# A two-block fp32 kernel: a transfer order, three instruction orders and four DRAM sums are moved

## The chip, the cores and the metric

The kernel runs on one core of one Trainium2 chip. The metric is the device time of one execution in microseconds, here the median of three runs.

## The reference

Two transformer-like blocks work on 256 tokens of width 2048, in fp32. Cut to its products:

```python
# block 1
proj = rmsnorm(x) @ w_in                  # 2048 x 8200
y = concat(mlstm(proj[...]), hgrn2(proj[...]))
h = x + y @ w_out
h = h + sigmoid(rmsnorm(h) @ w_pg) * (p @ w_pe)
x = rmsnorm(h)
# block 2
proj = rmsnorm(x) @ w_in_2                # 2048 x 9216: u, v, q, k, v_att, g_a, g_b
y_a, y_b = spatial_gating(u, v), stick_breaking_attention(q, k, v_att)
merged = sigmoid(g_a) * (y_a @ w_up_a) + sigmoid(g_b) * (y_b @ w_up_b)
x = x + merged @ w_o
hid = rmsnorm(x) @ w_ffn_in               # 2048 x 11264, then silu(gate) * up
x = x + (silu(gate) * up) @ w_ffn_out
x = x + sigmoid(rmsnorm(x) @ w_ple_gate) * (p_2 @ w_ple)
```

## The kernel before, in words

**Pieces.** All weights stream once through the core, in 848 numbered pieces. A piece is 256 rows by 512 columns of a weight (512 KB). Each piece passes three engines: ScalarE rounds it into `whi` (`split_hi`, L928, or `s_hi`, L1177), VectorE makes the rest `wlo = piece - whi` (L1876, or `s_lo`, L2556), and TensorE multiplies with high and low parts of the activations. A standard piece (`piece`, L1359 and L1364) is 8 matmuls on `whi` and 4 on `wlo`, for all 256 tokens. `whi` and `wlo` are rings of four pieces, `raw` is a ring of eight: ScalarE can be at most four pieces ahead of TensorE, and a load can start when the VectorE step that last read its place is done (`lo_ready`).

**Groups.** Most of the gates of block 2 and of the FFN input (12 groups: 0 to 2 in the merge, 3 to 11 in the FFN) are multiplied in a Strassen-like form of seven products of half size, M1 to M7, of four pieces each. The order is M1, M2, M7, M5, then M6 and M3 mixed, then M4. A piece of these has 4 matmuls on `whi` (L1724) and 2 on `wlo` (L1728). Standard pieces are mixed in.

**Where their weights come from.** M1's four pieces come into `r1` in two loads of 1 MB (L774). M5's come into the same `r1`, over M1's, in two loads of 1 MB (`fifth`, L780), from sums that lie in DRAM. M2, M7 and M3 take single 512 KB loads into four half-slots (L788): `b21`, `seventh` (sums from DRAM) and `b22`. M6's piece is `r1` plus `b22`, added on VectorE two pieces ahead (`s_sum`, L2551). M4's piece is `r1` plus `b21`: GpSimd issues an accumulating DMA into `r1` for it (L898) once M6's low part of that quarter is made.

**The order of the loads.** SyncE issues all loads in one order. For the second half it is the list `PLAN.loads`, sorted by (`free`, `need`): the piece whose `wlo` must be made first, and the piece that needs it. SyncE waits for each `free` in turn. `plan_s_loads` (L259 to L271) writes the entries of the groups.

**DRAM sums.** 48 sums of two weight tiles (1 MB each), four per group, are made in DRAM. SyncE issues a copy of the first term (L671, in `copies_for_sums`, ahead of the first load whose `need` reaches the entry of `SUM_AT`), GpSimd an accumulating DMA of the second (L882, in `add_in_dram`, once TensorE has used as many pieces as the entry says). Sums 0 to 39 are spread over pieces 24 to 269. Sums 40 to 43 stand at `g_plan + 1 + 4 * i` (pieces 277, 281, 285, 289) and 44 to 47 at `g_out + 11 + 6 * i` (419, 425, 431, 437). `g_plan` is 276, `g_out` 408, `g_ffn` 440. Group 3 starts at piece 458. Sums 40 to 47 belong to groups 10 and 11.

**The other places.** `ml_cols` on TensorE (L1484 to L1498) makes four small transposes and then spreads four rows over 128 partitions, two matmuls for each of two PSUM banks, with an operand of four partitions (L1497); VectorE reads both banks in `ml_weights`. On VectorE, the step at weight piece `L0 + 30` multiplies one half of the HGRN2 output by its norm (L2251, in front of the HGRN2 steps of the other half), and `u_product` (L2592, L2595) multiplies an up-projection with its gate, three pieces after the last piece of the slab.

Of the kernel before, what the change touches and what calls it, by code (L numbers as in the profile page):

```python
# [39 lines left out]
S = 256  # L40
# [82 lines left out]
class Plan:  # L123
# [129 lines left out]
    def plan_s_loads(self, groups):  # L253

        n = self.halves
        for c in groups:
            at = lambda i: self.s_at[(c, *S_ORDER[i])]
            for h in range(2):
                free = {0: self.g_plan + 9, M_GROUPS: self.g_block}.get(c)  # L259
                free = self.s_at[c - 1, "M4", 2 * h + 1] if free is None else free  # L260
                self.loads.append((free, self.s_at[c, "M1", 2 * h], "r1", h, c))
                self.loads.append((self.s_at[c, "M1", 2 * h + 1], self.s_at[c, "M5", 2 * h], "fifth", h, c))
            for i, (m, q) in enumerate(S_ORDER):
                for what, first, last in (("b21", "M2", "M2"), ("b22", "M6", "M3"), ("seventh", "M7", "M7")):
                    if m == first:
                        slot = RAW // 2 + n % 4
                        need = at(i - S_LEAD if m == "M6" else i)
                        self.loads.append((self.last_use[slot], need, "half", slot, (c, what, q)))
                        self.half[c, what, q] = (slot, 16 * (n // 4 + 1))
                        self.last_use[slot] = self.s_at[c, last, q]  # L270
                        n += 1  # L271
        self.halves = n
# [42 lines left out]
def two_blocks_kernel(nc, A, out):  # L315
    PLAN = Plan()
    SLABS, FIRST, S_AT = PLAN.slabs, PLAN.first, PLAN.s_at
    AUX = plan_aux()
    ctx = ExitStack()
    with ctx:  # L320
# [143 lines left out]
        summed = nc.dram_tensor("summed", (4 * S_GROUPS, P, 4 * COLS), F32, kind="Internal").ap()  # L464
        SUM_AT = [int(24 + SUM_STEP * i) for i in range(int(116 // SUM_STEP) + 1)] + [144 + 8 * i for i in range(7)]
        SUM_AT += [199 + int(5.4 * i) for i in (0, 1, 2, 3, 8, 9, 10, 11, 12, 13)]
        SUM_AT += [PLAN.g_plan + 1 + 4 * i for i in range(4)]
        SUM_AT += [PLAN.g_out + 11 + 6 * i for i in range(4 * S_GROUPS - len(SUM_AT))]

        acc = ctx.enter_context(nc.psum_tensor("acc", [P, 4, COLS], F32))  # L470
# [353 lines left out]
        def _(pool):  # L824
# [60 lines left out]
            for i, (name, n) in enumerate(POWS):  # L885
                add_in_dram(len([g for g in SUM_AT if g <= SUMS_UPTO.get(name, 0)]))
                if name == "qk0":

                    pool.wait_ge(sem("ws_loaded"), 16)
                    pool.affine_select(out=wsT[:, :, :], in_=wsT[:, :, :], compare_op=ALU.is_ge, fill=0.0, base=0,  # L890
                                       pattern=[[0, 8], [1, P]], channel_multiplier=-1).then_inc(sem("ws_masked"), 1)
                if name in ("ffn", "ple"):
                    for c in range(M_GROUPS) if name == "ffn" else range(M_GROUPS, S_GROUPS):
                        add_in_dram(len([g for g in SUM_AT if g < S_AT[c, "M6", 0]]))
                        for m, (what, before) in S_DMA.items():
                            for q in range(4):
                                pool.wait_ge(lo_ready, S_AT[c, before, q] + 1)
                                pool.dma_start(r1[:, q], s_weights(c, what, q), accum_op=ALU.add).then_inc(sem(f"r1_added{q}"), 16)  # L898
                if name == "ffn":
                    add_in_dram(len(SUM_AT))  # L900
                pool.wait_ge(pow_in, i + 1)
                pool.tensor_tensor(rstd[:, i, 0:n], var[:, i, 0:n], minus_half[:, 0:n], ALU.pow).then_inc(pow_out, 1)

# [418 lines left out]
        def _(pe):  # L1322
# [161 lines left out]
            def ml_cols():  # L1484
                u = AUX[("atr", 0)]
                pe.wait_ge(sem("ml_em"), 1)
                free(u)
                for x, row in ((0, 1), (1, 5)):
                    for t in range(T):
                        ins = pe.transpose(bank(u)[:, x * 8 + t * 4:x * 8 + t * 4 + 4], hrow[:, row, t * P:(t + 1) * P],  # L1490
                                           ident[0:4, 0:4])
                ins.then_inc(aux_full, 1)
                for i in range(2):
                    u = AUX[("bc", i)]
                    free(u)
                    for h in range(2):
                        ins = pe.matmul(bank(u)[:, h * S:(h + 1) * S], sel[:, 2 * i + h, :], hrow[:, 3, :], start=True, stop=True)  # L1497
                    ins.then_inc(aux_full, 1)  # L1498

            def ml_scores():  # L1500
                pe.wait_ge(sem("ml_qk"), 2)
# [21 lines left out]
            for s in range(16):  # L1523
                n = FIRST["A"] + s
                for p in range(8):
                    w = s * 8 + p
                    if w == 0:
                        first_piece()
                    else:
                        if s == 0:  # L1530
                            pe.wait_ge(sem("x_lo"), p + 1)
                        piece(n, p, actA, p * PK, p == 7)
                    if p == (5 if s == 1 else 2) and s - 1 in A_TRANSPOSED:
                        tr_slab(s - 1)
                    for half, L0 in enumerate(HG_START):
                        if w == L0 - 3:
                            hg_diag(half)
                        n_level, odd = divmod(w - L0, 2)
                        if 0 <= n_level < 8 and not odd:
                            hg_level(half, n_level)  # L1540
                        if w == L0 + 18:
                            hg_flip(half)
                        if w == L0 + 20:
                            hg_pv(half)
                    if (s, p) == (9, 4):
                        ml_gates()
                    if (s, p) == (9, 7):
                        ml_gates_by_token()
                    if (s, p) == (10, 4):
                        ml_gates_tr()  # L1550
                    if (s, p) == (10, 7):
                        ml_cols()
                    if (s, p) == (11, 4):
                        ml_scores()
                    for h in range(4):
                        if w == 95 + h:
                            ml_pv(h)
                    if (s, p) == (14, 4):
                        pe.wait_ge(sem("yb_ready"), 2)
                        for i in range(4, 8):  # L1560
                            transposes(("yT", i), ob, 2 * i - 8)
                    if (s, p) == (15, 2):
                        pe.wait_ge(sem("ya_ready"), 1)
                        for i in range(2):
                            transposes(("yT", i), hA, 2 * i)
# [298 lines left out]
        def _(dve):  # L1864
# [335 lines left out]
            for s in range(16):  # L2200
                for p in range(8):
# [22 lines left out]
                    for half, L0 in enumerate(HG_START):  # L2224
                        if w == L0 - (7 if half else 5):
                            hg_forget(half)
                        if w == L0 - (5 if half else 3):
                            hg_cumsum(half)
                        if w == L0 - 1:
                            hg_queries(half)  # L2230
                        if w == L0 + 1:
                            hg_diagonal(half)
                        n, odd = divmod(w - L0, 2)
                        if not odd:
                            if 0 <= n - 1 < 8:
                                hg_mul(half, n - 1)
                            if 0 <= n < 8:
                                hg_sub(half, n)
                        if odd and 0 <= n - 2 < 8:
                            hg_take(half, n - 2)  # L2240
                        if w == L0 + 21:
                            hg_flipped(half)
                        if w == L0 + 24:
                            hg_output(half)
                        if w == L0 + 27:
                            dve.wait_ge(sem("ss_hB"), half + 1)
                            variance(f"hB{half}", HG_E)
                        if w == L0 + 30:
                            powered(dve, f"hB{half}")
                            x = ob[:, :, half * 512:(half + 1) * 512].rearrange("p t (h c) -> p t h c", h=4)  # L2250
                            link(dve.tensor_tensor(x, x, per_head(f"hB{half}").unsqueeze(3).to_broadcast([P, T, 4, P]), ALU.mult))  # L2251
# [351 lines left out]
            for kind, g, *x in PLAN.merge:  # L2603
# [24 lines left out]
                        gate_taken(PLAN.ffn_slab[role, j, 0])  # L2628
                for j in range(4):
                    for role in ("uA", "uB"):  # L2630
                        if g == slab_end(role, j) + (2 if slab_end(role, j) in PLAN.block_end else 3):
                            u_product(role, j)
                for c in range(M_GROUPS):
                    if g == S_AT[c, "M2", 3] + 3:
# [216 lines left out]
```

## Time and profile before

| | us |
|---|---|
| median of 3 runs (1892.97 to 1895.27) | 1894.41 |
| the profiled execution | 1893.05 |
| its span, first to last instruction | 1891.3 |
| TensorE matmul busy | 1877.2 (99%) |
| VectorE busy | 1471.8 (78%) |
| ScalarE busy | 1140.8 (60%) |
| moved by DMA | 535.95 MB, mean 283 GB/s |

The rows of the trace are times from the start of the span. Matmuls overlap: each is listed with 0.38 us, though the next begins 0.216 us later. So what TensorE loses is read from the distance between starts.

### The profile page before, as it was taken

Reading aid. Unit: us, or ns where it says so; the run is one execution under the profiler, and the core shown is the slowest. Engines: PE = TensorE matmul, PEld = TensorE weight load, DVE = VectorE, ACT = ScalarE, POOL = GpSimd, SP = SyncE. Lnnn points to the kernel's source line nnn. Section 1 sums busy time; section 2 is a strip of 40 time slices with the busy share of each in tenths; the row PEclk is TensorE's granted clock in tenths of the full one; section 3 lists DMA queues with packets and bytes.
Section 4 is the critical chain, followed back from the end, with each engine's and each line's share of the span. In section 5 each row is a group of like instructions: output and inputs, shape, how many; then the busy total and the mean of one; then the engine's idle time right before and its main releaser. Section 6 shows DMA issues by size and latency. Waiting matters only on the chain.

```text
span 1891.3 us, 23371 instructions
## 1 busy us (share of the span) xinstructions
PE 1877.2 (99%) x9018; PEld 1641.9 (87%) x9018; DVE 1471.8 (78%) x1591; ACT 1140.8 (60%) x1417; POOL 130.4 (7%) x156
## 2 busy tenths in 40 slices
PE   9999999999999999999999999999999999999998
PEld 8888888888888888888888888888888888888887
DVE  6889776655666677778888657988998999898865
ACT  7556445555566556566766455666766676666553
POOL 4000011000001100000000000000000000000000
PEclk9999999999999999999999999999999999999999
DMA  9799898999989879998797886788878887987653
GB/s 392 267 284 310 274 309 272 330 347 327 309 290 312 271 269 299 321 315 278 295 313 247 330 256 239 254 311 284 276 254 320 280 271 257 327 260 249 219 188 130
DMA packets 86815, 535.95 MB, mean 283 GB/s; under 512 B 10416, under 2 KB 11184, under 8 KB 40752
## 3 DMA queue, kind: packets, MB, share of 16 engines
q1 hardware_dynamic: 72736, 458.69, 63.3%
q0 software_dynamic: 13824, 75.50, 20.6%
q8 instruction: 72, 1.18, 0.2%
q10 hardware_dynamic: 144, 0.26, 0.0%
q14 instruction: 39, 0.32, 0.0%
HBM read 529.69 MB, written 105.38 MB: 336 GB/s over the span
## 4 chain that ended last, share of the span: by engine, by line
PE 90%; DVE 5%; DMA 3%; issue 1%; ACT 1%; POOL 0%; SPq 0%; ACTq 0%; DVEq 0%; POOLq 0%
PE acc L1359 44%; PE acc L1364 22%; PE aux L1724 12%; PE aux L1728 6%; DVE wlo L2556 2%; PE aux L1338 2%; DMA ple<-in_w_ffn_in 1%; DVE wlo L1876 1%; PE aux L1431 1%; DVE ple L2551 1%; DMA ple<-in_w_in 1%; DMA raw<-summed 1%; PE aux L1805 0%; ACT whi L928 0%; ACT whi L1177 0%
## 5 line engine op out<-in xcount | busy, mean ns | idle before, releaser
L1876 DVE TENSOR_TENSOR wlo<-raw,whi 128x1024 fp32r<-128x1024 f32 x512 | 623.8, 1226 | 296.4 <-ACT whi L928 288.4
L928 ACT ACTIVATE whi<-raw 128x1024 fp32r<-128x1024 f32 x511 | 534.0, 1054 | 449.8 <-PE acc L1364 414.1
L1359 PE MATMUL acc<-whi,actA_hi 128*128 128x512 f32 x892 | 344.0, 386 | 0.7 <-ACT whi L928 0.7
L1359 PE MATMUL acc<-whi,actA_lo 128*128 128x512 f32 x892 | 339.1, 380 | 0.0
L1359 PE MATMUL acc<-whi,actB_hi 128*128 128x512 f32 x796 | 304.5, 383 | 0.2 <-DVE actB_lo L2673 0.2
L1359 PE MATMUL acc<-whi,actB_lo 128*128 128x512 f32 x796 | 301.7, 379 | 0.0
L1177 ACT ACTIVATE whi<-ple 128x1024 fp32r<-128x1024 f32 x192 | 201.0, 1055 | 139.4 <-PE acc L1364 55.6
L2556 DVE TENSOR_TENSOR wlo<-ple,whi 128x1024 fp32r<-128x1024 f32 x192 | 230.2, 1220 | 31.3 <-ACT whi L1177 28.5
L1364 PE MATMUL acc<-wlo,actA_hi 128*128 128x512 f32 x892 | 229.1, 379 | 0.0
L1364 PE MATMUL acc<-wlo,actB_hi 128*128 128x512 f32 x796 | 204.4, 379 | 0.0
L2556 DVE TENSOR_TENSOR wlo<-raw,whi 128x1024 fp32r<-128x1024 f32 x144 | 174.2, 1220 | 30.6 <-ACT whi L1177 28.9
L1359 PEld LDWEIGHTS acc<-whi,actA_hi 128*128 128x128 f32 x892 | 169.1, 190 | 25.5 <-issue 2.0
L1177 ACT ACTIVATE whi<-raw 128x1024 fp32r<-128x1024 f32 x144 | 152.0, 1055 | 64.3 <-PE acc L1364 36.5
L1364 PEld LDWEIGHTS acc<-wlo,actA_hi 128*128 128x128 f32 x892 | 168.9, 189 | 24.2
L1359 PEld LDWEIGHTS acc<-whi,actA_lo 128*128 128x128 f32 x892 | 169.2, 190 | 23.4 <-issue 0.5
L1359 PEld LDWEIGHTS acc<-whi,actB_hi 128*128 128x128 f32 x796 | 150.5, 189 | 21.6 <-DVE actB_lo L2673 1.0
L1364 PEld LDWEIGHTS acc<-wlo,actB_hi 128*128 128x128 f32 x796 | 150.4, 189 | 21.6 <-DVE wlo L1876 0.3
L1359 PEld LDWEIGHTS acc<-whi,actB_lo 128*128 128x128 f32 x796 | 150.6, 189 | 20.6
L1724 PE MATMUL aux<-whi,actB_hi 128*128 128x512 f32 x360 | 136.8, 380 | 0.8 <-ACT whi L1177 0.8
L1724 PE MATMUL aux<-whi,actB_lo 128*128 128x512 f32 x360 | 136.4, 379 | 0.0
L1728 PE MATMUL aux<-wlo,actB_hi 128*128 128x512 f32 x360 | 107.4, 380 | 0.9 <-DVE wlo L2556 0.8
L1724 PE MATMUL aux<-whi,actA_hi 128*128 128x512 f32 x216 | 83.0, 384 | 0.0
(366 smaller groups left out, 2377.0 us busy)
## 6 DMA issues: line engine op xcount, KB each, us to landing
raw<-in_w_in SPq DMA_DIRECT2D x108, 1024.0 KB, 7.3
raw<-in_w_ffn_out SPq DMA_DIRECT2D x44, 1024.0 KB, 6.9
summed<-in_w_ffn_in POOLq DMA_DIRECT2D x36, 1024.0 KB, 11.6
raw<-in_w_ffn_in SPq DMA_DIRECT2D x72, 512.0 KB, 7.9
ple<-summed SPq DMA_DIRECT2D x24, 1024.0 KB, 4.9
raw<-summed SPq DMA_DIRECT2D x48, 512.0 KB, 5.4
ple<-in_w_ffn_in SPq DMA_DIRECT2D x18, 1024.0 KB, 6.9
ple<-in_w_ffn_in POOLq DMA_DIRECT2D x36, 512.0 KB, 9.9
```

The costliest lines, as they stand in the source:

```text
L928: act.activation(whi[:, g % RING], raw_piece(g), ACT.Copy).then_inc(hi_ready, 1)
L1177: act.activation(whi[:, g % RING], s_source(c, m, q), ACT.Copy).then_inc(hi_ready, 1)
L1338: ins = pe.transpose(bank(u)[:, c * S + t * P:c * S + (t + 1) * P], src[:, t, (c0 + c) * P:(c0 + c + 1) * P], ident[:, :])
L1359: pe.matmul(acc2(n)[:, t, :], act[x][:, k + c, t * P:(t + 1) * P], woven(whi, g, c), start=(p == 0 and c == 0 and x == 0), stop=False)
L1364: ins = pe.matmul(acc2(n)[:, t, :], act[0][:, k + c, t * P:(t + 1) * P], woven(wlo, g, c), start=False, stop=(last and c == PK - 1))
L1431: ins = pe.matmul(bank(u)[:, c], Kp[n % 2][:, c], Qp[n % 2][:, c], start=True, stop=True)
L1724: pe.matmul(o, lhs(x, q * PK + k), woven(whi, g, k), start=(q == 0 and k == 0 and x == 0 and not onto), stop=False, skip_group_check=onto)
L1728: ins = pe.matmul(o, lhs(0, q * PK + k), woven(wlo, g, k), start=False, stop=(q == 3 and k == PK - 1), skip_group_check=onto)
L1876: dve.tensor_tensor(wlo[:, g % RING], raw_piece(g), whi[:, g % RING].bitcast(F32), ALU.subtract)\
L2551: dve.tensor_tensor(x, x, half_slot(c, S_ADDEND[m], q), ALU.add).then_inc(sem("s_sum"), 1)
L2556: dve.tensor_tensor(wlo[:, g % RING], s_source(c, m, q), whi[:, g % RING].bitcast(F32), ALU.subtract)\
```

## The change

Five edits. M5's load may start after M2's piece of the same half and no more after M1's. Sums 40 to 43 leave the first merge pieces: the last eight sums now stand at `g_out + 11 + 6 * i`, i = 0 to 7 (pieces 419, 425, 431, 437, 443, 449, 455, 461), and GpSimd makes those below `g_ffn` ahead of the FFN's norm and the other four ahead of group 3's M4. The second pair of row-spreading matmuls goes one piece later. The norm of the HGRN2 output goes from `L0 + 30` to `L0 + 31`. The product of `uB` 2 goes from three to five pieces after its slab.

```diff
-                self.loads.append((self.s_at[c, "M1", 2 * h + 1], self.s_at[c, "M5", 2 * h], "fifth", h, c))
+                self.loads.append((self.s_at[c, "M2", 2 * h + 1], self.s_at[c, "M5", 2 * h], "fifth", h, c))
...
-        SUM_AT += [PLAN.g_plan + 1 + 4 * i for i in range(4)]
         SUM_AT += [PLAN.g_out + 11 + 6 * i for i in range(4 * S_GROUPS - len(SUM_AT))]
...
                 if name == "ffn":
-                    add_in_dram(len(SUM_AT))
+                    add_in_dram(len([g for g in SUM_AT if g < PLAN.g_ffn]))
...
-                for i in range(2):
-                    u = AUX[("bc", i)]
-                    free(u)
-                    for h in range(2):
-                        ins = pe.matmul(bank(u)[:, h * S:(h + 1) * S], sel[:, 2 * i + h, :], hrow[:, 3, :], start=True, stop=True)
-                    ins.then_inc(aux_full, 1)
+
+            def ml_rows_spread(i):
+                u = AUX[("bc", i)]
+                free(u)
+                for h in range(2):
+                    ins = pe.matmul(bank(u)[:, h * S:(h + 1) * S], sel[:, 2 * i + h, :], hrow[:, 3, :], start=True, stop=True)
+                ins.then_inc(aux_full, 1)
...
                     if (s, p) == (10, 7):
                         ml_cols()
+                        ml_rows_spread(0)
+                    if (s, p) == (11, 0):
+                        ml_rows_spread(1)
...
-                        if w == L0 + 30:
+                        if w == L0 + 31:
                             powered(dve, f"hB{half}")
...
-                        if g == slab_end(role, j) + (2 if slab_end(role, j) in PLAN.block_end else 3):
+                        last = slab_end(role, j)
+                        if g == last + (2 if last in PLAN.block_end else 5 if (role, j) == ("uB", 2) else 3):
                             u_product(role, j)
```

## Rows read from the trace of the kernel before

**Rows 1.** The page: TensorE's busy time; queues, their packets, MB, share of 16 engines

```profile
PE 1877.2 (99%) x9018; PEld 1641.9 (87%) x9018; DVE 1471.8 (78%) x1591; ACT 1140.8 (60%) x1417; POOL 130.4 (7%) x156
...
q1 hardware_dynamic: 72736, 458.69, 63.3%
q0 software_dynamic: 13824, 75.50, 20.6%
```

**Rows 2.** Chain of work around the row spreading: start us, us, what

```profile
274.28 1.83 PE aux L1497 x8
276.11 3.43 PE acc L1359 x8
...
280.59 1.73 PE acc L1359 x8
```

**Rows 3.** Busy time of the engines by stretch, granted clock, DMA share, GB/s

```profile
276.00:280.00 4.00, 4.00 (x12) 3.15 (x12) 3.96 (x11) 0.00 (x0) 0.00 (x0) 0.57 1.00 262
```

**Rows 4.** Timeline of VectorE, the HGRN2 norm and what follows

```profile
158.79 1.22 DVE L2251 TENSOR_TENSOR hg_v<-hg_v,rstd 128x1024 f32<-128x1024 f32 x1
...
164.68 1.22 DVE L1876 TENSOR_TENSOR wlo<-raw,whi 128x1024 fp32r<-128x1024 f32 x1 [0.34 <-ACT whi L928]
```

**Rows 5.** Timeline of TensorE there

```profile
161.46 1.16 PE L1431 MATMUL aux<-hg_qd,hg_kd 128*128 128x128 f32 x8 [0.75 <-DVE hg_kd L2027]
```

**Rows 6.** Timeline of VectorE, the end of group 2

```profile
1025.93 1.23 DVE L2595 TENSOR_TENSOR gate<-gate,merge_gate 128x1024 f32<-128x1024 f32 x1
1027.30 1.23 DVE L2556 TENSOR_TENSOR wlo<-ple,whi 128x1024 fp32r<-128x1024 f32 x1
```

**Rows 7.** Timeline of TensorE there

```profile
1028.58 0.70 PE L1728 MATMUL aux<-wlo,actB_hi 128*128 128x512 f32 x2 [0.79 <-DVE wlo L2556]
```

**Rows 8.** Timeline of TensorE, group 0 (M7, then M4's last piece)

```profile
861.05 0.38 PE L1359 MATMUL acc<-whi,actB_hi 128*128 128x512 f32 x1
...
870.44 0.38 PE L1359 MATMUL acc<-whi,actB_hi 128*128 128x512 f32 x1
...
901.18 0.48 PE L1724 MATMUL aux<-whi,actB_hi 128*128 128x512 f32 x1 [0.79 <-ACT whi L1177]
```

**Rows 9.** Timeline of ScalarE, group 0: first piece of M7, last of M4

```profile
863.26 1.06 ACT L1177 ACTIVATE whi<-raw 128x1024 fp32r<-128x1024 f32 x1 [4.64 <-DMA raw<-summed]
...
900.07 1.06 ACT L1177 ACTIVATE whi<-ple 128x1024 fp32r<-128x1024 f32 x1 [3.68 <-DMA ple<-in_w_in]
```

**Rows 10.** Stretches as in Rows 3: group 0's loads, then those of group 3

```profile
805.00:858.00 53.00, 53.00 (x259) 46.67 (x258) 38.13 (x47) 33.28 (x42) 3.25 (x4) 1.00 0.99 318
...
1168.00:1186.00 18.00, 18.00 (x85) 15.78 (x84) 14.26 (x15) 10.78 (x9) 0.00 (x0) 1.00 0.88 345
1186.00:1192.00 6.00, 6.00 (x32) 5.25 (x31) 5.35 (x6) 4.60 (x5) 0.00 (x0) 1.00 0.70 236
1192.00:1204.00 12.00, 12.00 (x59) 10.53 (x58) 9.61 (x10) 8.07 (x9) 0.00 (x0) 1.00 0.90 319
...
1210.00:1215.00 5.00, 5.00 (x25) 4.38 (x24) 4.77 (x5) 3.22 (x4) 0.00 (x0) 1.00 0.06 24
```

**Rows 11.** Timeline of ScalarE, group 3: the third piece of M7

```profile
1200.49 1.06 ACT L1177 ACTIVATE whi<-raw 128x1024 fp32r<-128x1024 f32 x1 [0.19 <-DMA raw<-summed]
```

**Rows 12.** Timeline of TensorE, the same piece

```profile
1205.35 0.38 PE L1724 MATMUL aux<-whi,actB_hi 128*128 128x512 f32 x1
```

**Rows 13.** Line L788 from 1200.5 to 1200.8: group 3's first `b22` load

```profile
L788 SPq DMA_DIRECT2D raw<-in_w_ffn_in x1: 333/333/333, 1200.6 to 1200.6; - x1
...
DMA to landing us min/median/max: 7.0/7.0/7.0
```

**Rows 14.** Timeline of VectorE, group 3: M6's first sum

```profile
1210.43 1.22 DVE L2551 TENSOR_TENSOR ple<-ple,raw 128x1024 f32<-128x1024 f32 x1
```

**Rows 15.** Chain of work, group 3: the last accumulating DMA for M4

```profile
1225.97 10.77 DMA ple<-in_w_ffn_in
```

**Rows 16.** What ScalarE waited for: us in total, times, longest

```profile
ACT whi L1177 <- DMA ple<-in_w_ffn_in: 26.5, 19, 4.0
```

## The prediction

> **What bounds the kernel now.** I read the page first, then what TensorE waited for, then the chain and the stretches. TensorE is busy 1877.2 of 1891.3 us [rows 1]; the matmuls follow each other 0.216 us apart (8 in 1.73, [rows 2]), and nearly everything that another engine does is hidden behind them. So only time in which TensorE has no matmul, or a slow one, can be won: 14 us of gaps and a few us of slow matmuls. The changed lines sit at four such places. The other thing to see is how full the 16 DMA engines are: where loads, sums and accumulations meet they are busy all the time (0.99 from 805 to 858, [rows 10]), and there a weight comes late. An edit that moves transfers must be judged by what stands in the queue at the new place.
>
> **The row spreading.** The piece behind it starts at 276.11 and the next at 280.59: 4.48 us for 12 matmuls, where 12 x 0.216 = 2.59 is normal [rows 2]. The granted clock is 0.57 from 276 to 280, that is half of these four microseconds and more at 1.2 instead of 2.4 GHz, and it fell right behind 1.83 us of matmuls on a four-partition operand, in which TensorE never stood still [rows 2, 3]. Split in two, each half has a full piece of 12 dense matmuls before the other. Bounds: 1.89 won if the clock stays up, 1.9 lost if it falls behind each half. I take 1.8 won (one more change of shape costs some 0.1). VectorE reads the second bank three pieces later, so the later half makes nobody late.
>
> The Trainium skill (TensorE: Matmul & The Clock Gate, Part 1) says that the clock falls back after idle time of the engine. This trace differs: no gap stands ahead of the fall. By that rule alone the split changes nothing here, and the sum would be 1.8 us higher.
>
> **The HGRN2 norm.** VectorE does L2251 (1.22 us) in front of the products that TensorE waits for; TensorE idles 0.75 us, 0.9 with its refill [rows 4, 5]. One piece later the same 1.22 us lies in front of the next level's low part, where VectorE has 0.34 us idle [rows 4] and some 0.5 us in hand. I take 0.8 won; bounds 0 (the wait goes to the next level) and 0.9. The other half's norm moves by one piece as well; in both places over 2 us of slack follow, so I cost it at nothing (1.22 at most if that cover is gone).
>
> **The product of uB 2.** Its two VectorE steps end at 1027.16, then the low part of M4's last piece is made, 0.79 us too late for TensorE (about 1.0 with the restart) [rows 6, 7]. Five pieces after, they stand behind that low part and the next one. But the piece itself came by DMA only at about 1025; its own path leaves 0.25 us in hand. So between 0 and 1.0 is won; I take 0.6, since the loads below make it a little later.
>
> **Group 0 without the sums.** From 861.05 to 870.44 TensorE does one standard piece (2.59) and four of M7 (1.30 each), and 0.2 of switches are in every group: 9.39 - 7.78 = 1.6, so 1.5 lost. ScalarE waited 4.64 us for M7's first load [rows 8, 9]. The four copies and four accumulations that go away are large. By the page q0 takes 0.206 x 1891.3 = 390 us for 75.5 MB, 5.16 us per MB, so 5.4 for one accumulation of 1.05 MB; q1 takes 2.6 per MB, 2.7 for a copy [rows 1]. Together 4 x 8.1 = 32 us of the 16 engines leave a stretch of 53 us that was full [rows 10]. M7 is then in time: 1.5 won (bounds 1.2 and 1.6). At M4's last piece TensorE lost 0.79 us at once and about 1.9 with the restarts behind it [rows 8]; the accumulating DMA there takes as long as in group 3 (10.8, [rows 15]), where about 1.0 is lost with the low parts on time. VectorE will be less behind: 0.4 won (bounds 0 and 1.5).
>
> Sum of what is won: 1.8 + 0.8 + 0.6 + 1.5 + 0.4 = 5.1.
>
> **The sums at their new place.** The output product keeps four sums as before. The last four now meet the start of group 3: accumulations at pieces 449, 455 and 461, the last two at about 1179 and 1191, a copy at 1169. M7's loads are issued from 1192 on. Added ahead of its third load: the copy 2.7, the accumulation of 455 5.4, that of 461 5.4 (both queues are served in turn), some 2 left from 449: 15.5. Free in the old profile: 0.12 x 18 + 0.30 x 6 + 0.10 x 12 = 5.2 [rows 10]. M5's second load no longer stands in front: 2.7 less. So this load, landed at 1200.49, comes 7.6 us later, and with 1.06 for ScalarE the piece is ready at 1209.1, where TensorE wants it at 1205.35 [rows 11, 12]: 3.8 lost. Below, nothing is lost if the accumulations run faster than their average; the nearest case is group 0 with 1.5, in a fuller queue but with a shorter pile behind it. I take 2.5, and 0.9 more at M4, since M6's `b22` comes late as well. Bounds 0 and 6.
>
> The Trainium skill (DMA: Bandwidth & Descriptors, Anatomy of one DMA) fits an accumulating (GpSimd-issued) DMA with about 2 us and the bytes at 436 GB/s: 2.4 us of moving, not 5.4. By that the pile is 6 us smaller and group 3 loses nothing, 3.4 us less in the sum; the page of the profile speaks against it.
>
> **M5's loads behind M7's.** The list is sorted by `free`, so M5's first load goes between the second and third of M7, its second behind M7's fourth. No wait is added for SyncE, as its neighbours wait for the same steps. In groups 1 to 10 this gives up DMA time: of 1186 to 1192 (group 3) the engines were busy 0.70, with these loads [rows 10]. About 4 us of their work now lies in front of M7's third piece, of the standard pair and of `b22`. M7's third piece has room: ready at 1201.5, wanted at 1205.35 [rows 11, 12]. `b22` has less: landed at 1200.6 + 7.0 = 1207.6, first used by VectorE at 1210.43 [rows 13, 14], 2.8 us in hand, against 3.5 to 4.5 later. So the M6 sums come about 0.1 to 1.4 us late (I worked out the same for groups 1 to 10; the gap at 1210 to 1215, busy 0.06, is what fills up [rows 10]). VectorE is full there, so M4's accumulating DMAs are issued late by as much, and those are already at the edge: 19 waits of ScalarE in the FFN groups, 26.5 us in sum, mostly hidden by the ring [rows 16]. Slack of TensorE behind them is 0 to 0.7 us. That gives 0.9 in group 1, 0.7 in 5 and 7, 0.5 in 9, 0.9 in 10 and 0.3 in the rest: 4.0 lost. Bounds: 0, if the DMA engines catch up in their gaps, and 9, if every group pays its full delay.
>
> **Sum.** -5.1 + 3.4 + 4.0 = +2.3 us against the profiled execution: 1893.05 + 2.3 = 1895.4. That execution lay 1.36 us under the median, so the median is 1894.41 + 2.3 = 1896.7.
>
> **Rivals.**
> 1. Faster: the transfers fit in. The DMA engines have about a tenth to a third free in most stretches, and one group has twelve pieces from M2 to `b22`'s use. Then only about 0.6 is lost: 1894.41 - 5.1 + 0.6 = 1889.9. For it: 0.06 at 1210. Against: 2.8 in hand and 3.5 or more of delay.
> 2. Slower, one mechanism: late `b22` sets the FFN groups. From a delay of over 3.5 us in its landing on, each group passes 0.5 to 1.5 us to M4's last piece, 9 in sum, with 5 in group 3 and 5.1 won: 1894.4 + 8.9 = 1903.3. For it: M4's last piece waits for DMA now. Against: some groups have up to 0.7 us of room.
> 3. The clock falls all the same (the skill's rule on idle time, above): the forecast without 1.8, 1898.5.
> 4. The order does only half of what its name says, as M5's first load is still ahead of M7's third: this is in the forecast; were it fully behind, M7 would gain nothing in groups 1 to 10.
>
> **How the numbers follow.** What a measurement of this kernel can tell from no change is about 0.2%, 3.8 us. Chances: forecast 0.40, rival 1 0.27, rival 2 0.23, rival 3 0.10. The forecast's own range is 1893 to 1900. Under 1890.6 lies most of rival 1 and little else: faster 0.25. Over 1898.2 lie rival 2, half of rival 3 and a sixth of the forecast: slower 0.35. Same 0.40. The range of 8 in 10 reaches from rival 1 nearly to rival 2: 1889.0 to 1902.5.
>
> **What would show it.** The piece at 276 in 2.6 us with clock 1.00; no idle before L1431 at 160; no DMA wait of over 1 us before group 0's M7; DMA share near 1 from 1168 to 1210 and a TensorE gap at group 3's M7; L2551 waiting for `raw` loads in groups 1 to 10 and longer gaps at M4's last pieces. The forecast is wrong if group 3's M7 is on time, or if L2551 never waits.

## The result and the profile after

The changed kernel takes 1916.65 us (median of 4 runs, 1914.19 to 1918.77); the kernel before took 1894.16 us beside it (4 runs). The ratio is 1.0118 (95% interval 1.0101 to 1.0136): 22.5 us slower, where 1896.7 was forecast and 1902.5 was the upper end. Timed again later on another occasion, the same kernel takes 1908.46 us beside 1894.14: 14.3 us slower (e8 below). I come back to the 8 us between these two; the cause of the loss is the same in both.

The profiled execution has a span of 1916.9 us. Its page, against [rows 1]:

```profile
PE 1888.0 (98%) x9018; PEld 1641.2 (86%) x9018; DVE 1470.3 (77%) x1591; ACT 1133.4 (59%) x1417; POOL 130.8 (7%) x156
...
q1 hardware_dynamic: 72736, 458.69, 62.1%
q0 software_dynamic: 13824, 75.50, 20.3%
```

Same instructions, same packets, same MB: only the order differs. TensorE's loss is spread over the groups. What ScalarE and VectorE, which prepare its pieces, waited for (engine, line, what ended the wait: us in total, times, longest), after and then before:

```profile
ACT whi L1176 <- DMA raw<-summed: 55.3, 32, 4.5
ACT whi L1176 <- DVE ple L2554: 43.6, 34, 2.1
ACT whi L1176 <- DMA ple<-in_w_ffn_in: 38.2, 18, 4.5
...
DVE ple L2554 <- DMA raw<-in_w_ffn_in: 0.8, 1, 0.8
```

```profile
ACT whi L1177 <- DMA ple<-in_w_ffn_in: 26.5, 19, 4.0
ACT whi L1177 <- DVE ple L2551: 22.5, 17, 2.1
...
ACT whi L1177 <- DMA raw<-summed: 13.5, 18, 4.6
```

`raw<-summed` is M7's loads: the product that the new order was to help waits four times as long as before. The last line of the first fence is what the forecast had put its loss on, `b22` coming late for VectorE: one wait of 0.8 us.

ScalarE's timeline shows where (start, us, line, idle before and what ended it): group 0, then M4's last piece of group 2, group 3 and group 6.

```profile
862.00 1.06 ACT L1176 ACTIVATE whi<-raw 128x1024 fp32r<-128x1024 f32 x1 [2.12 <-DMA raw<-summed]
865.92 1.06 ACT L1176 ACTIVATE whi<-raw 128x1024 fp32r<-128x1024 f32 x1 [2.87 <-DMA raw<-summed]
...
1031.51 1.06 ACT L1176 ACTIVATE whi<-ple 128x1024 fp32r<-128x1024 f32 x1 [3.97 <-DMA ple<-in_w_in]
...
1208.07 1.06 ACT L1176 ACTIVATE whi<-raw 128x1024 fp32r<-128x1024 f32 x1 [4.46 <-DMA raw<-summed]
...
1213.02 1.06 ACT L1176 ACTIVATE whi<-raw 128x1024 fp32r<-128x1024 f32 x1 [2.60 <-DMA raw<-summed]
...
1406.81 1.06 ACT L1176 ACTIVATE whi<-raw 128x1024 fp32r<-128x1024 f32 x1 [2.13 <-DMA raw<-summed]
1410.56 1.06 ACT L1176 ACTIVATE whi<-raw 128x1024 fp32r<-128x1024 f32 x1 [2.69 <-DMA raw<-summed]
```

The same two pieces of group 6 (M7's third and fourth) before; here ScalarE waits for TensorE, not for a load:

```profile
1391.15 1.06 ACT L1177 ACTIVATE whi<-raw 128x1024 fp32r<-128x1024 f32 x1 [0.24 <-PE aux L1728]
1393.74 1.06 ACT L1177 ACTIVATE whi<-raw 128x1024 fp32r<-128x1024 f32 x1 [1.53 <-PE acc L1364]
```

Why the third load is late is seen in SyncE's timeline after, the issues of group 6. L787 is M7's load (512 KB), L779 M5's (1 MB):

```profile
1399.21 0.33 SPq L787 DMA_DIRECT2D raw<-summed  x1
1399.63 0.38 SPq L779 DMA_DIRECT2D ple<-summed  x1
1400.34 0.32 SPq L787 DMA_DIRECT2D raw<-summed  x1
```

M7's third load, from issue to landing, after:

```profile
L787 SPq DMA_DIRECT2D raw<-summed x1: 319/319/319, 1400.3 to 1400.3; - x1
...
DMA to landing us min/median/max: 10.2/10.2/10.2
```

and before:

```profile
L788 SPq DMA_DIRECT2D raw<-summed x1: 320/320/320, 1385.4 to 1385.4; - x1
...
DMA to landing us min/median/max: 5.3/5.3/5.3
```

The stretches say what was given up. Before (columns as in [rows 3]; the last two are DMA share and GB/s), M5's loads of group 6 were issued in the third of these (the first two lie ahead of group 3):

```profile
1150.00:1160.00 10.00, 10.00 (x48) 8.75 (x47) 8.80 (x11) 4.23 (x4) 0.71 (x1) 1.00 0.35 127
1160.00:1168.00 8.00, 8.00 (x39) 7.00 (x38) 7.76 (x7) 5.61 (x6) 0.00 (x0) 1.00 0.35 133
...
1376.00:1383.00 7.00, 7.00 (x36) 6.15 (x35) 7.00 (x7) 4.66 (x6) 0.00 (x0) 1.00 0.70 233
1383.00:1393.00 10.00, 10.00 (x50) 8.77 (x49) 8.38 (x10) 7.03 (x8) 0.00 (x0) 1.00 0.92 323
```

After, the DMA engines idle for three quarters of the 8 us ahead of M7's loads (from 1398 on) and are busy 0.78 and then 1.00 of the time behind. The other rows are the clock's two places and group 3, against [rows 3, 10]:

```profile
220.00:224.00 4.00, 4.00 (x20) 3.73 (x20) 3.75 (x9) 0.00 (x0) 0.00 (x0) 0.58 1.00 197
276.00:280.00 4.00, 4.00 (x18) 2.98 (x18) 3.25 (x6) 0.96 (x2) 0.00 (x0) 1.00 0.98 260
1150.00:1168.00 18.00, 18.00 (x87) 15.86 (x86) 15.28 (x18) 9.37 (x12) 1.54 (x2) 1.00 0.89 291
1168.00:1186.00 18.00, 18.00 (x85) 15.79 (x85) 14.24 (x13) 12.44 (x12) 1.63 (x2) 1.00 0.97 331
1192.00:1204.00 12.00, 12.00 (x61) 10.58 (x60) 9.56 (x10) 8.63 (x10) 0.81 (x1) 1.00 1.03 312
1204.00:1216.00 12.00, 9.21 (x40) 6.77 (x39) 5.78 (x6) 4.90 (x5) 0.00 (x0) 1.00 1.00 394
...
1390.00:1398.00 8.00, 8.00 (x41) 7.03 (x40) 8.00 (x10) 5.45 (x7) 0.00 (x0) 1.00 0.24 99
1398.00:1408.00 10.00, 10.00 (x50) 8.79 (x49) 6.70 (x8) 5.82 (x7) 0.00 (x0) 1.00 0.78 253
1408.00:1418.00 10.00, 9.28 (x42) 7.42 (x41) 8.00 (x8) 6.30 (x7) 0.00 (x0) 1.00 1.00 413
```

Set against each other piece by piece, the two profiled executions differ by 25.6 us: 0.1 up to the merge (where gains of 2.0 meet 1.7 of clock and 0.4 of a wait at 44 us), -0.1 in group 0, 5.3 in groups 1 and 2, 0.15 in the output product, 4.9 in group 3, 15.2 in groups 4 to 10.

### The profile page after: what moved, and what is told of

The parts are those of the page before. It is cut to its first block, busy times and chain, and to the rows that moved or that the text cites. A ratio compares the mean times of both kernels' runs of the same rounds, so it can differ in the third digit from the quotient of the medians.

```text
span 1916.9 us, 23371 instructions
## 1 busy us (share of the span) xinstructions
PE 1888.0 (98%) x9018; PEld 1641.2 (86%) x9018; DVE 1470.3 (77%) x1591; ACT 1133.4 (59%) x1417; POOL 130.8 (7%) x156
## 4 chain that ended last, share of the span: by engine, by line
PE 68%; DVE 15%; DMA 11%; ACT 3%; issue 2%; POOL 0%; SPq 0%; ACTq 0%; DVEq 0%; POOLq 0%
PE acc L1358 38%; PE acc L1363 19%; DVE wlo L2559 9%; DMA raw<-summed 5%; PE aux L1727 4%; DMA ple<-in_w_ffn_in 3%; DVE ple L2554 2%; DVE wlo L1879 2%; PE aux L1731 2%; PE aux L1337 2%; ACT whi L1176 1%; DMA raw<-in_w_in 1%; DMA ple<-in_w_in 1%; ACT whi L927 1%; PE aux L1430 1%
```

## Experiments

A number to compare runs by: the time from the first matmul of the standard piece ahead of M7 to the first of M5, read from TensorE's timeline. It is 10.36 us when nothing waits (two pieces of 2.59, four of 1.295). Each row is one execution, the first of its kernel: for e5 and e13 that was the fastest (1898.97 and 1889.96 us), for the changed kernel, e7 and e11 the slowest (1918.77, 1912.45 and 1904.58 us).

```
group                    0      1      2      3      4      5      6      7      8      9     10
before               11.98  10.36  10.36  10.36  10.36  10.36  10.36  10.36  10.36  10.36  10.36
after                11.57  12.34  12.99  14.20  10.59  11.85  11.62  10.36  11.85  11.92  12.00
e8 after again       10.62  12.09  10.54  13.76  10.48  11.58  10.69  10.36  12.27  10.50  11.46
e1 M5's order only   10.36  11.04  11.31  10.36  10.88  11.74  10.51  10.36  11.03  12.16  11.78
e2 sums only         10.36  10.36  10.36  18.67  10.36  10.36  10.36  10.36  10.36  10.36  10.36
e7 M5's first load   12.56  11.99  12.04  10.36  10.36  12.83  10.65  10.36  11.40  10.76  11.76
e3 small orders      11.55  10.36  10.36  10.36  10.36  10.36  10.36  10.36  10.36  10.36  10.36
e4 M5's loads back   10.36  10.36  10.36  18.59  10.36  10.36  10.36  10.36  10.36  10.36  10.36
e11 first, 512 KB    10.73  11.47  12.47  10.36  10.36  12.22  10.36  10.36  11.17  10.60  10.36
e12 first load back  10.36  10.36  10.36  15.17  10.36  10.36  10.36  10.36  10.36  10.36  10.36
e5, e6, e9, e13      10.36  10.36  10.36  10.36  10.36  10.36  10.36  10.36  10.36  10.36  10.36
```

The second number is M7's third load from issue to landing, mean over groups 1, 2 and 4 to 10: 5.9 us before, 9.6 after, 9.0 in e8 and e1. Below, a difference in us is one of medians; the ratio was worked out apart from it and lies up to 0.1% beside the quotient of the medians.

**One part each (e1 to e4).** e1 has this edit alone, e2 the moved sums with their loop bound, e3 the three small orders; e4 is the changed kernel with this edit undone:

```
-                self.loads.append((self.s_at[c, "M1", 2 * h + 1], self.s_at[c, "M5", 2 * h], "fifth", h, c))
+                self.loads.append((self.s_at[c, "M2", 2 * h + 1], self.s_at[c, "M5", 2 * h], "fifth", h, c))
```

> The kernel before with M5's loads later and nothing else. Theory A (M5's loads push M7's third load and b22 back in every group): groups 1, 2 and 4 to 10 lose what they lost in the changed kernel, 20.5 us in sum, and groups 0 and 3 some 1 to 2 us each: 1914 to 1919 us. ScalarE waits 2.6 us or more for M7's third load in nearly every group. Rival B (the moved sums carry the loss, since a queue that is once behind stays behind): only my forecast's 4 us, 1898 us, and M7 in time from group 4 on.

Measured: 1908.82 us (4 runs, 1907.06 to 1914.03), ratio 1.0087 (1.0069 to 1.0105), 14.4 us slower. Less than the 20.5 us I expected, but the largest part by far, and M7's third load takes 8.4 to 10.0 us to land in each of groups 1 to 10, with no sum moved. Rival B falls. Group 0 gains instead of losing: with M5's loads out of the way its M7 is in time although the sums still run there.

> The kernel before with the four sums moved and nothing else. Theory A: group 0 wins 1.5 to 1.9 us at M7, group 3 loses 0 to 4 us, nothing changes from group 4 on: 1892.5 to 1896.5 us. Rival B: groups 4 to 10 lose 1 to 2 us each, 1908 us or more.

Measured: 1898.56 us (10 runs), ratio 1.0023 (1.0014 to 1.0033), 4.2 us slower, above my range. Group 0's M7 wins 1.6 us and its M4 0.5; group 3's M7 loses 8.3, twice my upper end; M7 in groups 4 to 10 is in time, so rival B falls.

> The kernel before with the three small orders and nothing else. By the forecast's terms 1.8 + 0.8 + 0.6 = 3.2 us less, 1891.2 us, with the clock at 1.00 at 276 us. Rival C (a fall of the clock is not removed but appears elsewhere, as at 220 us in the changed kernel): 1.4 us less, 1893.0, and a stretch of granted clock under 0.8 between 216 and 290 us. The queues are as before: groups 1 to 11 within 0.3 us of the kernel before, but for group 2's last piece (0.6 to 1.0 us less).

Measured: 1891.78 us (10 runs), ratio 0.9993 (0.9983 to 1.0002): 2.6 us less, not told from no change by the interval. The clock is 1.00 at 276 and 0.57 at 220. That is the sign that rival C named, but e1 and e2, which keep the pair together, have the fall at 220 as well as the one at 276: it has not moved there. Group 2 is 1.1 us better, as expected; group 3 is 0.8 and group 7 0.4 better too, with nothing changed in them, so that much is scatter. The parts are taken apart in the next section.

> The changed kernel with M5's loads back at their old place: small orders and moved sums together. Theory A: 20 us or more less than the changed kernel, 1890 to 1895 us, and M7 in time in groups 1, 2 and 4 to 10. Rival B: at most 4 us less than the changed kernel, 1912 us.

Measured: 1896.92 us (median of 10 runs; 1895.99 to 1897.28 but for one of 4044.03 us, which isn't explained), ratio 1.0017 (1.0007 to 1.0026), above my range. Undoing one line of the change takes 11.5 us off e8 and 19.7 off the first measurement. Where the sums meet group 3, ScalarE stands for 10 us ahead of M7's first piece:

```profile
1204.37 1.06 ACT L1176 ACTIVATE whi<-raw 128x1024 fp32r<-128x1024 f32 x1 [10.06 <-DMA raw<-summed]
```

**Which of M5's two loads (e5 to e7), and the changed kernel once more (e8).** From the kernel before, the free step of the load, `h` = 0 or 1:

```
e5   self.s_at[c, "M2", 3]                            both behind M7's fourth load
e6   self.s_at[c, "M2" if h else "M1", 2 * h + 1]     only the second, behind M7's fourth
e7   self.s_at[c, "M1" if h else "M2", 2 * h + 1]     only the first, between M7's second and third
```

> The kernel before with both of M5's loads behind M7's fourth load. Theory A (two separate losses: M7's third load behind M5's first, and `b22` behind both): the M7 part of e1_m5_only's loss goes (7.6 us in groups 1 to 10) and the rest stays: 1899 to 1903 us, M7 at 10.36 us with its neighbours in all of groups 1 to 10. Rival D (the loss only moves on, since M5's first load is now the late one): TensorE waits in front of M5's first piece by 1 us or more in most groups, 1906 us or more.

Measured: 1904.02 us (4 runs, 1898.97 to 1907.12), ratio 1.0047 (1.0028 to 1.0065), 9.9 us slower. The median is above my range and the scatter is wide. In the profiled execution, the fastest, M7 is in time everywhere, and now `b22` and its like are what VectorE waits for:

```profile
ACT whi L1177 <- DVE ple L2551: 41.4, 34, 2.1
ACT whi L1177 <- DMA raw<-summed: 10.4, 15, 2.5
DVE ple L2551 <- DMA raw<-in_w_ffn_in: 7.7, 8, 1.4
DVE ple L2551 <- DMA raw<-in_w_in: 3.6, 3, 1.4
```

So the mechanism on which the forecast built exists, but in this order and not in that of the change. M5's first piece has over 3 us in hand in every group: rival D falls.

> The kernel before with only M5's second load moved (behind M7's fourth). Theory A: M7 in time in groups 1 to 10, `b22` some 3 us later: 2 to 5 us lost, 1896 to 1900 us. Rival D: the same 14 us as with both, 1906 us or more.

Measured: 1891.79 us (10 runs), ratio 0.9989 (0.9979 to 0.9998): 2.4 us faster where I expected 2 to 5 us lost. 1 MB more ahead of `b22` costs next to nothing (0.4 us from group 1 on in the profile), and group 0's M7 (1.6 us) is won by the second load alone.

> The kernel before with only M5's first load moved (between M7's second and third). Theory A: M7's third piece late in most groups, 5 to 9 us lost, 1899 to 1904 us, more than with the second load alone. Rival E (it is the bytes in front of `b22` that count, whichever load they are): the same as e6_m5_second_half within 2 us.

Measured: 1906.59 us (4 runs, 1905.15 to 1912.45), ratio 1.0069 (1.0052 to 1.0086), 12.5 us slower: the first load alone carries nearly all of e1. (With e6's gain the two loads add up to 10.1 us, against 14.4 together; e1 and e7 have four runs each, and what of this is scatter is open.) The bytes ahead of `b22` are the same in e6 and e7; rival E falls.

> The changed kernel once more, on the same chip as its parts. If the parts add up (14.4 + 4.2 - 2.6 = 16.0 us) it takes 1910.5 us here; if the 22.5 us measured first hold on another chip as well, 1916.7 us, and then the parts make each other worse by some 6 us.

Measured: 1908.46 us (4 runs, 1907.86 to 1908.99), ratio 1.0073 (1.0058 to 1.0088). The parts add up within their scatter: 14.4 + 4.2 - 2.6 = 16.0 against 14.3.

**Bytes or place (e11, e13).** e7 with M5's first load cut. This is e13's edit, with 128 of the 2048 columns; e11 does the same with 1024:

```
-                sp.dma_start(r1[:, 2 * h:2 * h + 2].rearrange("p q k c -> p (q k c)"), summed[4 * c + 2 + h])\
-                    .then_inc(sem(f"r1_loaded{h}"), 16)
+                dst = r1[:, 2 * h:2 * h + 2].rearrange("p q k c -> p (q k c)")
+                n = 4 * COLS if h else 128
+                sp.dma_start(dst[:, 0:n], summed[4 * c + 2 + h][:, 0:n]).then_inc(sem(f"r1_loaded{h}"), 16)
```

> e7_m5_first_half with M5's first load cut to half of its bytes (512 KB; the second of its two products' weights isn't loaded, so that part of the output is computed from old weights); order, issue and waits are the same. Theory A (M7's third load waits for the bytes of the load ahead): its landing is 1.5 to 1.9 us earlier than in e7_m5_first_half and most of the loss at M7 goes, 1896 to 1901 us. Rival F (it is the place in the queue or the issue by SyncE that costs, whatever the size): the same as e7_m5_first_half, 1905 us or more.

Measured: 1900.40 us (7 runs, 1896.56 to 1904.58), 6.2 us less than e7. The time is where theory A had it, the landing is not: 8.4 us against 8.9, half a microsecond instead of 1.5 to 1.9. That alone decided nothing.

> e7_m5_first_half with M5's first load cut to 64 KB (128 columns of the 2048; the rest of these weights is old, so M5's part of the output is wrong); place, issue and waits are the same. From half of the bytes the third load of M7 landed only 0.5 us earlier, but the time was half-way back. Theory A (bytes ahead): with 64 KB ahead the third load takes 5.9 us from issue to landing as in the kernel before, and the time is 1892 to 1896 us. Rival F (the place, an issue or a fixed price of one more transfer there): the third load takes 8 us or more and the time stays at 1899 us or more.

Measured: 1892.68 us (10 runs), ratio 0.9996 (0.9987 to 1.0006). The third load takes 6.0 us on the mean; the transfer still stands in its place, and M7 is in time. What ScalarE waited for, in e7 and in e13:

```profile
ACT whi L1177 <- DMA raw<-summed: 45.5, 30, 3.8
```

```profile
ACT whi L1178 <- DMA raw<-summed: 13.3, 21, 2.1
```

With 64 KB, 512 KB and 1 MB ahead of M7's third load, that load takes 6.0, 8.4 and 8.9 us, in executions of 1889.96, 1904.58 and 1912.45 us; the medians of the kernels are 1892.7, 1900.4 and 1906.6 us. Rival F falls. That half the bytes cost most of the delay isn't explained. Nor do e11 and e13 tell waiting behind the load from sharing the DMA engines with it: they take its bytes away altogether.

**Both gains together (e9, e12).** e9 is e3 and e6 in one kernel; e12 is the changed kernel with M5's first load back.

> The kernel before with the three small orders and only M5's second load moved; M5's first load and the sums stay. If the two gains measured alone (2.6 and 2.4 us) add up, 1889.2 us; if they share group 0's M7 (they touch different lines, but both were timed within 0.1% of each other and of the noise), 1891 us.

Measured: 1889.94 us (9 runs, 1887.48 to 1891.32), ratio 0.9975 (0.9966 to 0.9985): 4.2 us faster than the kernel before, with an interval of 2.8 to 6.4. That is nearer to the sum of the two gains than to 1891, but the interval holds both.

> The changed kernel with M5's first load alone back at its old place. Theory A (this one load is the loss): 12 us or more less than the changed kernel on this chip, 1891 to 1896 us, with M7 at 10.36 us in groups 1, 2 and 4 to 10 and a loss of 4 to 8 us left at group 3's M7, from the sums. Rival B (the sums' queue): over 1900 us.

Measured: 1895.42 us (10 runs), ratio 1.0005 (0.9996 to 1.0014), 13.0 us less than e8. M7 is in time in groups 1, 2 and 4 to 10 and takes 15.17 us in group 3, 4.8 lost. Moving M5's first load back repairs the change down to its moved sums; e9 shows that these were not needed, since M5's second load frees group 0 already.

## Why the prediction was wrong

**M5's loads (forecast 4.0 lost, measured 14.4 in e1).** This is the step that failed. The forecast saw rightly that the first load goes between M7's second and third, and it put about 4 us of DMA work ahead of that third piece. By its own price of 2.7 us a transfer of 1 MB it is 2.7 there, and 5.4 ahead of `b22`; the third load landed 3.7 us later after the change, 3.1 in e8. Then it said "M7's third piece has room: ready at 1201.5, wanted at 1205.35". Three things were wrong in that sentence. First, 3.85 us of room was read in group 3 and taken for all groups; between the end of ScalarE's step and TensorE's first matmul the third piece had 2.1 us in group 1, 2.5 in group 5, 3.0 in group 8. Second, a room of 3.85 against a delay of 4 is no room: it should have been a coin's toss in each of ten groups, not "this is in the forecast" at no cost. Third, the delay was priced as if it ended with itself. When the third piece comes late, so does its low part, and the fourth starts another 0.5 us late behind it. In groups 2, 5, 8 and 9 TensorE then waits 1.0 to 1.2 us more, because VectorE has another step of 1.21 us to do (L2595 or L2722) before the fourth's low part. After group 2's M7 the kernel is 2.6 us later although the load itself made only 0.9 of it. In groups 1, 2 and 4 to 10 the M7 stretches lose 12.3 us in the first profile after (7.6 in e1, 6.7 in e8), the pieces from M5 to M3 2.9 (2.1, 1.9) and M4 5.4 (4.6, 3.2).

The loss was looked for at `b22` with 2.8 us in hand. The change hardly makes it late (0.8 us in one wait), and "if L2551 never waits" was the forecast's own sign of being wrong: TensorE, held up at M7, asks for it later too. Rival 2 names that mechanism and is wrong as well; rival 4 names the place ("M5's first load is still ahead of M7's third") and gives it no price.

At M4, where the forecast put its 4.0, e1 loses 4.6, and the end of its chain is there: in groups 1, 2 and 4 to 10 M4's accumulating DMAs are issued 0.7 to 1.1 us later behind M5's first piece than before. But they follow VectorE's low parts of M6, which are as much later though `b22` is in time. VectorE comes behind at M7 and in e1 idles at most 0.14 us from there to M6's last piece, so it can't catch up. That this share came out right is luck.

**The sums (forecast 1.5 + 0.4 won in group 0, 3.4 lost in group 3).** Alone, group 0 wins 1.6 and 0.5 (e2): right, and the 0.2 of switches that were taken off aren't there (10.36 us are two pieces of 2.59 and four of 1.295). Group 3 loses 4.9 in the changed kernel and 3.9 in e8, within the bounds of 0 and 6, though above 3.4. With M5's loads at their old place it loses 7.9 (e2) and 7.7 (e4). The price of an accumulation held (in e4, from 1150 to 1204, the 4.06 MB of them took 20.6 us of the 16 engines); the pile was counted too late. I charged 15.5 us of work from 1168 on and let the engines be free before it. In e4 they are not:

```profile
1150.00:1168.00 18.00, 18.00 (x85) 15.77 (x84) 15.24 (x13) 11.44 (x11) 0.81 (x1) 1.00 0.99 283
1168.00:1186.00 18.00, 18.00 (x87) 15.75 (x87) 16.07 (x16) 9.72 (x12) 0.81 (x1) 1.00 1.01 353
1186.00:1192.00 6.00, 6.00 (x31) 5.26 (x30) 4.61 (x5) 3.80 (x5) 0.81 (x1) 1.00 1.03 403
1192.00:1204.00 12.00, 7.07 (x33) 5.86 (x31) 3.11 (x4) 2.31 (x3) 0.00 (x0) 0.91 1.02 343
1204.00:1210.00 6.00, 4.43 (x14) 3.70 (x15) 4.55 (x5) 5.05 (x5) 0.00 (x0) 0.62 1.00 395
```

Free before the change from 1150 to 1204: 0.65 x 18 (by the stretches of before above), 0.12 x 18, 0.30 x 6 and 0.10 x 12 by [rows 10], 16.9 us. Added: 3 copies and 4 accumulations at my prices, 29.7. The 12.8 left over come near what M7's first load shows: against the pieces in front of it, it lands 10.1 us later in e2 and 11.5 in e4. Room takes 4.9 of that, and M7's first piece starts 5.3 us late in e2 and 6.7 in e4. The rest of the 8.3 and 8.2 there, 3.1 and 1.6, is the clock of TensorE, which fell at this wait (0.62 from 1204 to 1210 in e4): the first pieces behind it take up to 2.7 us instead of 1.3. The forecast had no such term. The sum over the whole stretch that fills up gives the size of the delay; the sum over its end does not.

In the changed kernel the same pile costs less, and e12 shows why: with M5's second load alone behind M7's fourth, group 3 loses 4.6. The forecast had counted 2.7 for this load; e12 gives 3.1 against e4. So moving the second load pays in group 3 as in group 0 (e6), and the first load gives nothing there that the runs show.

The Trainium skill (DMA: Bandwidth & Descriptors, Anatomy of one DMA) fits one GpSimd-issued DMA, not an accumulating one in particular; its price would have made the forecast's pile 6 us smaller and group 3 lose nothing. The trace goes with the page of the profile, 5.3 us of the 16 engines for an accumulation of 1.05 MB in e4, and not with 2.4.

**The row spreading (1.8 won).** The piece behind it takes 1.93 + 0.86 us, clock 1.00. Over the two pieces from 276 on, the profiles after, of e3 and of e4 are 1.3 to 1.4 us better than before: the second change of shape costs some 0.5 and not 0.1. The chain of work after:

```profile
275.87 0.97 PE aux L1497 x4
276.84 1.93 PE acc L1358 x8
278.76 0.86 PE acc L1363 x4
279.63 1.06 PE aux L1497 x4
280.69 1.92 PE acc L1358 x8
```

**The HGRN2 norm (0.8 won).** The wait of [rows 5] is gone, 1.0 us at this place. Of it 0.3 is given back by piece 54 (at 168 us) and 0.2 by piece 60 (at 187); what TensorE meets there isn't taken apart. So 0.5 is won. TensorE's first products without a wait, and VectorE's norm at its new place:

```profile
160.97 1.05 PE L1430 MATMUL aux<-hg_qd,hg_kd 128*128 128x128 f32 x8
```

```profile
162.81 1.23 DVE L2254 TENSOR_TENSOR hg_v<-hg_v,rstd 128x1024 f32<-128x1024 f32 x1
...
164.68 1.22 DVE L1879 TENSOR_TENSOR wlo<-raw,whi 128x1024 fp32r<-128x1024 f32 x1
```

**The product of uB 2 (0.6 won, between 0 and 1.0).** 1.06 us in e3 and 0.9 in e12, where the piece's own DMA lands in time; 0.15 in the changed kernel, where it does not (the 3.97 us wait in ScalarE's timeline above). M5's loads aren't the reason: e4 and e9 win no more than 0.16 and 0.15, with the first load at its old place. The bounds were right; what decides between their ends is that DMA's landing, which differs from run to run.

**Rival 3** falls: no fall of the clock is found at 276 in any of the six profiles with the split. In sum, the won part was forecast at 5.1 and is 4.7 when nothing else is moved (2.6 in e3, 2.1 of group 0 in e2). The lost part was forecast at 4.0 for M5's loads and 3.4 for the sums; alone they cost 14.4 (e1) and, in group 3, 7.9 (e2), of which the second load takes 3 back. Group 0's gain at M7 is 0.4 in the first profile after, 1.4 in e8 and 1.6 in e1.

## What to carry to other kernels

When a load is moved, list every transfer that it then overtakes or stands in front of, and read the room of each one in every repetition of the loop, not in one: a room that equals the delay within its scatter must be priced as lost. Idle DMA time ahead of a busy stretch is worth keeping for a load that has its buffer early; "later" only pays for a load whose early place is itself full. Where work is added to a queue, the sum must start where that work starts, and not only in front of the piece that is watched. A wait of TensorE long enough for its clock to fall costs more than the wait.

## What the runs showed of the hardware

The clock of TensorE falls from 2.4 to 1.2 GHz at two places in most profiles, and not in each execution. At 220 us, behind 2.6 us in which TensorE waited (there from 217 in every profile), it fell in 11 of 14 and cost 1.4 to 1.7 us; the profile of before is one of the three without, and 1.7 us of the difference between the two profiles is this; it may be why its time lay 1.4 us under the median. In e2, e4 and e12 it also fell in group 3, in or right behind the wait ahead of M7's first piece, which starts 5.3, 6.7 and 3.1 us late there. At 276, behind four matmuls on four partitions with no gap ahead (four small transposes on four partitions stand in front of them, with the split as well), it fell in 7 of the 8 profiles that keep them together and in none of the 6 with the split; the eighth is e5:

```profile
276.00:280.00 4.00, 4.00 (x21) 3.27 (x22) 2.82 (x5) 1.06 (x1) 0.00 (x0) 1.00 0.97 252
```

The Trainium skill (TensorE: Matmul & The Clock Gate, Part 1) has the clock fall after idle time. The trace agrees at 220 and in group 3, and differs at 276.

The changed kernel took 1916.65 us in one set of runs and 1908.46 in another, each within 5 us, while the kernel before took 1894.16 and 1894.14. Its third M7 load landed after 9.6 us in the one profile and 9.0 in the other. A kernel with room in front of its loads could hide such a difference, and one without would show it in each of ten groups; no run shows that this is the reason. Whether it belongs to the chip or to the placement of the data wasn't tried and stays open, as does why 512 KB ahead of a load delay it nearly as much as 1 MB.
